# Hybrid attention and recurrence block: heads of seven column tiles instead of eleven, and the gate tiles in a stage of their own, most of them by seven block products

## What is computed

```python
u    = rmsnorm(x, g_mix)
proj = u @ w_in                      # 2048 -> 11264 columns
sb_q, sb_k, sb_v, hg_q, hg_f, hg_i, hg_og, gate_a, gate_b = split(proj)
q, k = rmsnorm(heads(sb_q)), rmsnorm(heads(sb_k))
y_a  = stick_breaking_attention(q, k, heads(sb_v))        # 8 heads x 128
f    = lb + (1 - lb) * sigmoid(heads(hg_f))
o_b  = hgrn2(silu(hg_q), 1 - f, hg_i, log(f))             # 8 heads x 128
y_b  = rmsnorm(o_b) * silu(hg_og)
m    = sigmoid(gate_a) * (y_a @ p_a) + sigmoid(gate_b) * (y_b @ p_b)
h    = x + m @ w_o
out  = h + (silu(conv(gate)) * conv(val)) @ w_down        # of rmsnorm(h) @ w_up
```

## Time and profile before

| | us |
|---|---|
| three runs | 2849.4, 2849.91, 2850.65 (median 2849.91) |
| the profiled execution | 2850.21 |
| its span | 2848.7 |
| PE busy | 2833.0 (99%) |
| DVE busy | 1875.6 (66%) |
| ACT busy | 1181.6 (41%) |
| TensorE clock granted | 1.00 |

### The profile page before, as it was taken

How to read it: one execution, slowest core, us unless ns; L and a number is a source line. 1 busy time by engine, 2 the same in 40 slices (tenths; PEclk the granted TensorE clock), 3 DMA queues, 4 the chain that set the end, 5 groups by cost and what they waited for, 6 DMA issues and landing times.

```text
span 2848.7 us, 46207 instructions
## 1 busy us (share of the span) xinstructions
PE 2833.0 (99%) x16214; PEld 2491.5 (87%) x16214; DVE 1875.6 (66%) x3307; ACT 1181.6 (41%) x1581; POOL 281.3 (10%) x382
## 2 busy tenths in 40 slices
PE   8999999999999999999999999999999999999999
PEld 6888888888888888888889999999999999999998
DVE  6555454545454546544458978878888887887884
ACT  5333333232323233323345544545444544544444
POOL 1000101020200100000100111101111110111112
PEclk9999999999999999999999999999999999999999
DMA  4242425252433323444445656566655655656557
GB/s 159 81 138 86 146 85 148 93 154 87 113 99 94 102 87 109 150 141 143 143 160 152 144 135 140 134 138 135 135 139 134 139 135 137 136 135 139 135 136 166
DMA packets 157446, 367.48 MB, mean 129 GB/s; under 512 B 18224, under 2 KB 27824, under 8 KB 156848
## 3 DMA queue, kind: packets, MB, share of 16 engines
q1 hardware_dynamic: 112464, 274.46, 31.3%
q0 software_dynamic: 44768, 90.20, 18.0%
HBM read 303.77 MB, written 78.12 MB: 134 GB/s over the span
## 4 chain that ended last, share of the span: by engine, by line
PE 98%; DMA 1%; DVE 1%; ACT 0%; issue 0%; SPq 0%; DVEq 0%; ACTq 0%
PE bank L1490 15%; PE bank L1492 15%; PE bank L1491 15%; PE bank L1659 10%; PE bank L1661 10%; PE bank L1660 10%; PE bank L1694 6%; PE bank L1695 6%; PE bank L1696 6%; PE bank L1538 1%; PE bank L1523 1%; PE bank L1581 1%; PE bank L1569 1%; DMA w_raw<-wstream 0%; DMA x_in<-x_t 0%; PE bank L1517 0%
## 5 line engine op out<-in xcount | busy, mean ns | idle before, releaser
L1659 PE MATMUL bank<-v_hi,w_hi 128*128 128x256 f32 x2464 | 697.9, 283 | 1.4 <-issue 0.6
L1661 PE MATMUL bank<-v_hi,w_lo 128*128 128x256 f32 x2464 | 697.3, 283 | 0.0
L1660 PE MATMUL bank<-v_lo,w_hi 128*128 128x256 f32 x2464 | 697.3, 283 | 0.0
L746 ACT ACTIVATE w_hi<-w_raw 128x896 fp32r<-128x896 f32 (+1 forms) x528 | 444.9, 846 | 564.0 <-DVE w_raw L1281 388.0
L1288 DVE TENSOR_TENSOR w_lo<-w_raw,w_hi 128x896 fp32r<-128x896 f32 (+1 forms) x528 | 499.8, 952 | 100.8 <-ACT w_hi L746 98.4
L1490 PE MATMUL bank<-u_hi,w_hi 128*128 128x512 f32 x1408 | 555.4, 394 | 10.8 <-DVE u_lo L918 10.3
L1492 PE MATMUL bank<-u_hi,w_lo 128*128 128x512 f32 x1408 | 549.4, 390 | 0.0
L1491 PE MATMUL bank<-u_lo,w_hi 128*128 128x512 f32 x1408 | 549.0, 390 | 0.0
L892 DVE TENSOR_TENSOR w_lo<-w_raw,w_hi 128x1024 fp32r<-128x1024 f32 x240 | 292.7, 1222 | 302.1 <-ACT w_hi L551 299.0
L1659 PEld LDWEIGHTS bank<-v_hi,w_hi 128*128 128x128 f32 x2464 | 472.8, 192 | 4.7 <-issue 3.1
L1660 PEld LDWEIGHTS bank<-v_lo,w_hi 128*128 128x128 f32 x2464 | 472.9, 192 | 1.8 <-issue 0.2
(11 more groups left out here) (226 smaller groups left out, 3311.3 us busy)
## 6 DMA issues: line engine op xcount, KB each, us to landing
w_raw<-wslots SPq DMA_DIRECT2D x504, 256.0 KB, 2.7
w_raw<-wstream SPq DMA_DIRECT2D x240, 512.0 KB, 3.6
out_t<-stage POOLq DMA_DIRECT2D x168, 256.0 KB, 4.4
sums_scratch<-wfirst POOLq DMA_DIRECT2D x24, 448.0 KB, 11.7
w_raw<-sums_scratch SPq DMA_DIRECT2D x24, 448.0 KB, 3.3
gates_scratch<-g_out POOLq DMA_DIRECT2D x32, 256.0 KB, 3.0
g_in<-gates_scratch POOLq DMA_DIRECT2D x16, 512.0 KB, 4.0
x_in<-x_t SPq DMA_DIRECT2D x8, 512.0 KB, 10.1
```

The lines of the kernel that those rows point to most:

```text
L746: act.activation(w4_hi[ring][:, 0:width], w4_raw[ring][:, 0:width], ACT.Copy).then_inc(w4_hi_ready, 1)
L1659: nc.tensor.matmul(out, wh, xh, start=kp == 0 and half == 0, stop=False, skip_group_check=True)
L1660: nc.tensor.matmul(out, wh, xl_, start=False, stop=False, skip_group_check=True)
L1661: ins = nc.tensor.matmul(out, wl, xh, start=False, stop=kp == KP - 1, skip_group_check=True)
```

## The change

1. A head has 14 units (`HEAD_TILES = 7`). Its steps keep their positions 0 to 17; the sum of squares of the output moves from 18 to 20, its normalization from 19 to 21. Steps at positions 14 to 21 therefore fall on positions 0 to 7 of the next head: each engine's `phase1_body` first does the step 14 + p of the head before, then step p of its own. Behind head 7 they fall on the first gate units.
2. A gate stage follows the heads. Its first eight tiles run as before, 16 units of 24 matmuls, while DVE and ACT make the token sums `t_hi`, `t_lo` of `u` (positions `T_UNITS`).
3. The other 24 tiles run as 12 pairs of eight slots (`gate_slot`), 21 matmuls of 256 columns each. Even slots load ready sums (448 KB from `sums_dram`), odd slots load 256 KB from `wgates` and DVE makes the sums (`gate_sums`). The slots keep the ring of four; the sums of slot j + 2 are made at position j, the low part of slot j + 1 (`gate_lo`) after them. Five DVE steps behind a pair combine and store it (`gate_pair`).
4. The batches of accumulating DMAs hold 12 slots instead of 6 and there are six instead of four of them (48 gate slots and 24 of phase 4).
5. Splitting `y_raw` is moved into the last pair: `y_high(c)`, `y_low(0)` and `y_low(1)` between slots, `y_low(2)` and `(3)` behind them.

```diff
-HEAD_UNITS = 22
-HEAD_TILES = 11
+HEAD_UNITS = 14
+HEAD_TILES = 7
+GATES = 2 * KT
+GATE_TILES = 8
+GATE_PAIRS = (GATES - GATE_TILES) // 2
+PAIR_SLOTS = GATE_PAIRS * (KT // 2)
-NPRE, BATCH = 24, 6
+NPRE, NGATE, BATCH = 24, PAIR_SLOTS // 2, 12
...
+SUMSQ = [{2: "q", 4: "k", 20: "out"}, {6: "q", 7: "k", 21: "out"}]
+T_UNITS = [4, 5, 8, 9, 10, 11, 12, 13]
...
+            for j in range(PAIR_SLOTS):
+                n = START_P + j
+                sp_.wait_ge(unit_done, n + 1)
+                if j % 2 == 0:
+                    sp_.dma_start(w_raw[n % WSLOTS][:, 0:WC], sums_dram[j // 2, :, :]).then_inc(w_in_slot[n % WSLOTS], 16)
+                else:
+                    sp_.dma_start(w_raw[n % WSLOTS][:, 0:SC], wgates[j // 2, :, :]).then_inc(w_in_slot[n % WSLOTS], 16)
...
+            for turn in range(batches + 3):
+                if turn < HEADS:
+                    pool.wait_ge(unit_done, WSLOTS + turn * HEAD_UNITS + 10)
                 for stage_ in range(3, -1, -1):
+                    if 0 <= turn - stage_ < batches:
+                        first_sums(stage_, turn - stage_)
...
                     for p in range(HEAD_UNITS):
                         split_ahead(0, i, BODY1, hh * HEAD_UNITS + p)
+                        if not (isinstance(i, int) and hh == 0):
+                            head_steps(i, hh - 1, HEAD_UNITS + p)
+                        head_steps(i, hh, p)
...
+            for j in range(PAIR_SLOTS):
+                if j + 2 < PAIR_SLOTS and j % 2 == 1:
+                    gate_sums(j + 2)
+                if j + 1 < PAIR_SLOTS:
+                    gate_lo(j + 1)
+                else:
+                    split_lo(START2, START2 % WSLOTS)
+                if j >= KP and j % KP < 5:
+                    gate_pair(j // KP - 1, j % KP)
+                if j == PAIR_SLOTS - 5:
+                    y_low(0)
+                if j == PAIR_SLOTS - 2:
+                    y_low(1)
...
+                for w, x, b, half in PRODUCTS:
+                    out = bank[b0 + b][:, half * HALF:(half + 1) * HALF]
+                    wh, wl = (blocks(t, w) for t in (w_hi[slot], w_lo[slot]))
...
+                    nc.tensor.matmul(out, wh, xh, start=kp == 0 and half == 0, stop=False, skip_group_check=True)
+                    nc.tensor.matmul(out, wh, xl_, start=False, stop=False, skip_group_check=True)
+                    ins = nc.tensor.matmul(out, wl, xh, start=False, stop=kp == KP - 1, skip_group_check=True)
```

More of the change, by code:

```diff
@@ L697, in _, with gate_hi @@
[L697 removed]
+                assert steps.n == first + ACT_STEPS1, steps.n - first
+            steps.base, steps.n = 0, first + (HEADS // HEADS_PER_BODY - 1) * ACT_STEPS1
+            def gate_hi(j):
+                n = START_P + j
+                if j % 2 == 0:
+                    act.wait_ge(w_in_slot[n % WSLOTS], 16 * (n // WSLOTS + 1))
+                else:
+                    act.wait_ge(gw_sums, j // 2 + 1)
+                act.wait_ge(unit_done, n + 1)
+                act.activation(w_hi[n % WSLOTS][:, 0:WC], w_raw[n % WSLOTS][:, 0:WC], ACT.Copy).then_inc(w_hi_ready, 1)
@@ L700, in _, with gate_p1, high_sums, y_high @@
+            def gate_p1(k):
+                act.wait_ge(unit_done, gate_unit(k))
+                if k > 0:
+                    act.wait_ge(tile_out, 2 + TILES_G + GATE_TILES + 2 * k)
+                act.activation(gg_sum[:, 0:HALF], bank[gate_bank(k)][:, 0:HALF], ACT.Copy).then_inc(gp1_ready, 1)
+            def high_sums(kp):
+                act.wait_ge(gt_ready, kp + 1)
+                act.activation(t_hi[kp][:, :], t_raw[:, :], ACT.Copy).then_inc(t_hi_ready, 1)
             YC = GROUP * SEQ
-            for c in range(4):
+            def y_high(c):
+                if c == 0:
+                    steps.wait()
@@ L1201, in _ @@
+            split_lo(START2 + 1, (START2 + 1) % WSLOTS)
+            y_low(2)
+            y_low(3)
+            for q in range(5):
+                gate_pair(GATE_PAIRS - 1, q)
             step2 = steps.n
@@ L1572, in phase1_body @@
-                        if p == 7 + late:
-                            pe.wait_ge(tile_out, per(HEAD_TILES, 2 + 2 + 1))
-                            to_tokens()
-                        if p == 9 + 3 * late:
-                            pe.wait_ge(sp_lo_ready, per(1, 1))
-                            for b in range(NB):
-                                for b2 in range(b, NB):
-                                    for part in (sp_hi, sp_lo):
-                                        ins = nc.tensor.matmul(Z[b][:, b2 * P:SEQ],
-                                                               (ntri_r if b2 == b else nones_r)[:, :],
-                                                               part[:, ROW[b2]:ROW[b2 + 1]],
-                                                               start=False, stop=True, skip_group_check=True)
-                            ins.then_inc(c_done, 1)
@@ L1754, in slot_stream, with whole_slots @@
     return s
-def first_slots(slots):
-    a21, a12, a22, a11 = (slots[:NPRE, :, j * P:(j + 1) * P] for j in range(4))
+def whole_slots(slots):
+    a21, a12, a22, a11 = (slots[:, :, j * P:(j + 1) * P] for j in range(4))
     return np.concatenate([a12, a12, a22, a11, a21, a21, a11], axis=2)
```

819 lines of the change are left out of this document (498 added, 321 removed).

## The result

Four runs of the changed kernel took 2875.99 to 2881.19 us, median 2879.24; four of the kernel before 2848.79 to 2850.65, median 2849.65. The ratio is 1.0103, 95% interval 1.0085 to 1.0120. It is slower by 1%, where 2852 us and a range up to 2867 had been forecast.

What follows compares the result with a forecast made beforehand. PE's instruction costs were taken to bound the kernel, with next to no waits; -19.3 + 12.9 + 5.6 + 1.4 + 1.5 = +2.1 us on 2850.2 gave 2852 us, 8-in-10 range 2838 to 2867.

Steps and rivals of the forecast that it cites:

- The matmuls: PE, gate stage: 261.2 us of 512-wide matmuls go, 241.9 us of 256-wide ones come, -19.3 us.
- Rival D: Gate stage: half-wide matmuls cost 0.130 us instead of 0.120, so no saving on PE; 2871 us, chance 0.03.
- Step 9: Where a head follows a head: the inserted normalization makes PE wait 1.85 us for `sp_lo`, 7 times, +12.9 us.
- Rival A: Heads: PE does not wait for `sp_lo`; 2839 us, or 2832 without the ring's term too; chance 0.17.
- The ring: Gate pairs: odd slots' loads above 2.62 us delay even slots, 0.12 us on average, 47 loads, +5.6 us.
- Rival B: Gate pairs: loads of 2.9 us or more make the ring bind; 2860 us, 2873 at 3.2 us; chance 0.22.
- The pieces of y: Last pair: `y_low(0)` between low parts of slots 92 and 93 makes DVE late once, +1.4 us, bounds 0 and 3.
- POOL's batches: Heads: copies in DRAM slow weight loads, 9.3 us allowed for the nearest; +1.5 us for all six, bounds 0 and 10.
- rival C: Batches starve weight loads: at 15 us a load each costs 5.7 us; 2885 us, chance 0.10.
- The other overlapped steps: Heads, positions 14 and 16: 1.8 us of slack left at the nearest, `qk_ready`; no term, bound +1 us a head.
- The granted clock is full throughout and nothing here pauses PE long: Whole kernel, PE: the clock was left at full, with no term for a slower one.

Runs made afterwards that it cites:

- norm: Changed kernel with only DVE's normalization of the head before moved from position 7 of the next head to 9, behind `sp_lo`; 2868.41 us.
- nosums: Changed kernel without POOL's weight sums: 36 slots loaded straight from the input, no copies or accumulating DMAs, output lacks these sums; 2868.21 us.
- quiet: Changed kernel with PE's loop over head pairs cut behind unit 8 and DVE's ahead of position 10, lists no longer than before; 2866.76 us.
- act: Changed kernel with ACT's high part of the token sums issued one unit later, behind the high part of the next weights; 2876.05 us.
- split: Changed kernel with the same accumulating DMAs in twelve batches of six, two to a head, instead of six of twelve; 2871.76 us.
- straight: Changed kernel with PE's loop over pairs of heads written out, no jump; other engines keep their loops; 2899.60 us.
- rotate: Changed kernel with PE's loop over head pairs cut behind unit 8 and one pair more written out, leaving one jump; 2902.28 us.

## Why the prediction was wrong

- **The matmuls, -19.3: right.** The first matmul of each group of three, by line, in the window 912 to 1011 us (columns as in the earlier trace rows):

```profile
L1868 PE MATMUL bank<-t_hi,w_hi x156: 278/283/283, 912.0 to 1010.4; 128*128 128x256 f32 x156
...
L1868 PE MATMUL bank<-u_hi,w_hi x116: 280/283/387, 912.4 to 1009.3; 128*128 128x256 f32 x116
```

  Together 272 groups of three: 98.4 / (271 x 3) = 0.121 us each with the slots' waits in between, where 0.120 was used. Rival D is out. 261.2 us went and 248.9 came, waits and all, a gain of 12. By the prediction's estimate from the figures of the Trainium skill's page "TensorE: Matmul & The Clock Gate", section "Back-to-back issue gap", the same exchange would have been a loss of 46; this trace does not agree with it either.
- **Step 9, +12.9: right.** Seven waits of 1.7 us, 11.7 in all, and `norm` took them away. The end of the inserted piece and what it pushes back, on DVE's timeline of one head:

```profile
265.37 0.69 DVE L1267 TENSOR_TENSOR y_raw<-y_raw,og 128x512 f32 x1
265.98 0.68 DVE L1137 TENSOR_TENSOR pre<-bank,r_tok 128x512 f32<-128x512 f32 x1
...
271.69 1.49 DVE L1204 TENSOR_TENSOR sp_lo<-sp,sp_hi 128x1280 fp32r<-128x1280 f32 x1
```

  `sp_lo` ends at 273.18, PE starts at 273.23. Rival A is out (its lower figure, with the ring's term gone too, adds up to 2833.5, not 2832).
- **The ring, +5.6: a size.** The waits came where they should, at the start of even slots, 2.9 us in all. The 256 KB loads landed in 2.4 / 2.6 / 3.3 us against the limit of 2.62, a little better than the earlier trace rows. Rival B is out. **The pieces of y, +1.4:** 1.05 at slot 93. That the pairs' 7.0 is also the sum of these two terms is chance: 1.6 of it is the late second slot, 1.5 is spread within the slots.
- **POOL's batches, +1.5 with bounds 0 and 10: this step failed first.** It asked only whether the load nearest to its use lands in time. Weight loads beside a batch took up to 13.8 us (issued at 77.4), 12.9 (190.4) and 13.4 (300.9), above the 9.3 allowed, which is rival C in two heads (3.0 us at step 15) and in head 0 (1.2 us at step 13, then 6.8 us at half speed). That rival C's 2885 us lies near the measured 2879 is chance: these waits are 4.2 of its 34 us. But half of what the batches cost in waits (4.5 us) is at the loop's jumps, where they double the time until the next instructions are there. Without batches the kernel gains 11 us, so the term was too small by some 10.
- **"The other overlapped steps: no term": failed.** I followed waits between engines and not the loop's jump, which the change moved with the end of the head. Before, PE jumped behind a unit of 24 matmuls of 0.2267 us, and DVE in idle time. Now it jumps behind 24 matmuls of 64 columns, 2.8 us in all, in the middle of the recurrence's chain: 4.0 us for two jumps even without batches (`nosums`). `quiet` shows that place and batch together made the 8.5, and the slow clock behind them. The page that I should have weighed is the Trainium skill's "Runtime: NRT & Kernel Launch", section "Instruction fetch mechanics": a taken branch out of what is loaded must first fetch the target's page of instructions by DMA. The trace agrees: on the instruction queues 8 KB start at 402.88 and 16 KB at 404.56 us, at the start of and inside the changed kernel's idle stretch from 403.07 to 407.20. The page gives no time for it, and does not say that other DMAs lengthen it, which 2.0 against 4.1 us here do show.
- **The token sums: missing.** The prediction says nothing of them. Their work fits (with `act` DVE keeps up), but the order of ACT's list makes DVE and ACT wait in turn. The trace of `act` shows 7 us and one half-speed stretch going; its time alone wouldn't.
- **"The granted clock is full throughout and nothing here pauses PE long": failed.** 9.7 us, a third of the whole loss, is work done at 1.2 GHz behind or around the waits above. It came as an addition to waits that the sum had left out, and also once behind waits of 1.4 and 2.2 us (893 us). I read the clock only in a kernel that has no waits.

The failed steps are not independent: unpriced waits of 20 us brought 10 us of slow clock with them. That the range ended at 2867 came from bounding each term by its own landing times, with no case for the clock.

## What to carry to other kernels

When a change moves the end of a loop's body, look at what stands directly ahead of the jump on every engine: a jump is free behind long queued matmuls or in idle time, and cost 2 to 3 us an engine here in a dense chain, 3.5 to 7 with a burst of DMAs from GpSimd in flight. Look at all engines' jumps together, since one can hide another. In a kernel that PE bounds, allow for a stretch at half the clock behind a new wait (here it followed most waits of 2 us or more, and few shorter ones), and when work is added on two engines, check the order in both lists, not only the busy time.

## What was not expected of the hardware

- A loop's jump costs time on each engine: PE 2.0 and 2.1 us and DVE 3.1 without batches (`nosums`), and 3.5 to 4.3 and 5.6 to 6.9 while POOL issued the last of a turn's 48 DMAs, twelve copies of 448 KB. PE started 1.5 to 1.7 us behind the end of 16 KB on an instruction queue in either case.
- Making PE's list longer by 28 units or more ahead of it changed what PE's waits for nothing in the feed-forward stage cost: 8.0, 7.8 and 8.3 us in all in those three kernels, and 0.2 to 2.8 in the other kernels. The late matmul had moved from about the 30th to the 12th or 14th of the loop's body; the cause is left open.
- The granted clock fell behind PE's waits in stretches of 3.4, 6.8, 10.2 or 13.7 us, and not behind every one. In the fourteen traces, the first 20 us left out, it fell during or just behind 37 of 42 waits of 2 us or more, but only 12 of 102 of 1 to 2 us. The waits of 1.7 us for `sp_lo` left it at 1.00 in the changed kernel, but one or two of the seven were followed by a stretch in `act`, `nosums`, `split`, `straight`, `rotate` and `quiet` (172.10 to 175.51 us).
